# Forgetting attention beside a convolution's layer norm: mean from two partial sums, statistics at the end of their steps, gate exponential one step later

## The reference, cut to what matters

```python
u = a * jax.nn.sigmoid(g)
u = causal_depthwise_conv(u, conv_w, conv_b)              # 31 taps, 512 channels
u = jax.nn.silu(layer_norm(u, conv_ln_g, conv_ln_b))      # mean and variance over the channels
...
for i in range(S // Q_BLOCK):                             # forgetting attention, 8 heads of 64
    logits = q_i @ k[:kl].T * scale + cum[q0:kl, None] - cum[None, :kl]
    p = softmax(where(mask, logits, NEG_INF)); outs.append(p @ v[:kl])
...
return jnp.concatenate([u, att], axis=-1) @ w_out
```

## Time and profile before

| | us |
|---|---|
| median of 3 runs | 1816.08 |
| lowest, highest | 1813.85, 1817.47 |
| the profiled execution | 1815.37 |
| its span in the trace | 1813.6 |
| PE, DVE, ACT, POOL busy | 1773.4, 1029.9, 463.9, 1074.8 |

### The profile page before, as it was taken

The page is one execution under the profiler, slowest core; times in us unless marked ns, Lnnn a source line. Parts: engine busy times, 40 slices in busy tenths (PEclk is TensorE's granted clock), DMA queues, the critical chain, the costliest instruction groups (busy, mean ns, idle before and its releaser), DMA issues.

```text
span 1813.6 us, 22611 instructions
## 1 busy us (share of the span) xinstructions
PE 1773.4 (98%) x8364; PEld 1435.2 (79%) x8364; DVE 1029.9 (57%) x1194; ACT 463.9 (26%) x931; POOL 1074.8 (59%) x604
## 2 busy tenths in 40 slices
PE   9998999999999999999999999999999999999997
PEld 7775777788888877767888888887887888888886
DVE  5999355835252675175625262696766562616177
ACT  6427335401010222163201010212335320202011
POOL 7594452566666665434666666665344566666672
PEclk9999999999999999999999999999999999999999
DMA  6232221233333333211333333332222223333331
GB/s 241 70 100 64 70 82 47 79 96 93 102 95 93 98 100 93 82 47 59 93 98 99 93 94 103 93 93 82 70 70 59 82 93 99 98 93 95 102 93 47
DMA packets 46591, 161.44 MB, mean 89 GB/s; under 512 B 5232, under 2 KB 7792, under 8 KB 46384
## 3 DMA queue, kind: packets, MB, share of 16 engines
q1 hardware_dynamic: 45088, 157.31, 28.5%
q10 hardware_dynamic: 1424, 3.02, 0.5%
HBM read 158.21 MB, written 2.10 MB: 88 GB/s over the span
## 4 chain that ended last, share of the span: by engine, by line
PE 92%; DVE 4%; ACT 2%; issue 1%; POOL 1%; DMA 0%; SPq 0%; DVEq 0%; POOLq 0%; ACTq 0%
PE bank L406 21%; PE bank L407 21%; PE bank L408 21%; PE bank L454 3%; PE bank L455 3%; PE bank L456 3%; PE bank L474 1%; PE bank L476 1%; PE bank L475 1%; PE bank L1002 1%; PE bank L1038 1%; PE bank L1004 1%; PE bank L1003 1%; DVE bank L1773 1%; PE bank L1053 1%
## 5 line engine op out<-in xcount | busy, mean ns | idle before, releaser
L320 POOL TENSOR_TENSOR WL<-RAW,WH 128x1024 fp32r<-128x1024 f32 x291 | 740.8, 2546 | 24.3
L315 POOL TENSOR_SCALAR WH<-RAW 128x1024 fp32r<-128x1024 f32 x291 | 313.2, 1076 | 670.4 <-PE bank L408 363.0
L406 PE MATMUL bank<-AH,WH 128*128 128x512 f32 x848 | 332.6, 392 | 0.0
L408 PE MATMUL bank<-AH,WL 128*128 128x512 f32 x848 | 330.0, 389 | 0.0
L407 PE MATMUL bank<-AL,WH 128*128 128x512 f32 x848 | 330.0, 389 | 0.0
L406 PE MATMUL bank<-HH,WH 128*128 128x512 f32 x832 | 325.2, 391 | 0.0
L407 PE MATMUL bank<-HL,WH 128*128 128x512 f32 x832 | 324.0, 389 | 0.0
L408 PE MATMUL bank<-HH,WL 128*128 128x512 f32 x832 | 323.7, 389 | 0.0
L1428 ACT ACTIVATE TMP<-bank 128x512 f32<-128x512 f32 x96 | 57.3, 596 | 776.9 <-PE bank L408 739.1
L2049 DVE TENSOR_TENSOR HL<-TMP,HH 128x512 fp32r<-128x512 f32 x96 | 239.0, 2490 | 4.0 <-ACT HH L1433 0.7
L2055 DVE TENSOR_TENSOR Y<-Y,bank 128x512 f32<-128x512 f32 x72 | 49.5, 688 | 309.3 <-PE bank L408 309.3
(11 more groups left out here) (390 smaller groups left out, 2355.4 us busy)
## 6 DMA issues: line engine op xcount, KB each, us to landing
RAW<-wstream SPq DMA_DIRECT2D x291, 512.0 KB, 3.5
out<-Y SPq DMA_DIRECT2D x8, 256.0 KB, 2.2
X<-xT SPq DMA_DIRECT2D x3, 512.0 KB, 8.1
TMP<-memT ACTq DMA_DIRECT2D x1, 1024.0 KB, 7.2
MIX<-bands ACTq DMA_DIRECT2D x1, 768.0 KB, 4.6
RAW<-wstream SPq DMA_DIRECT2D x2, 256.0 KB, 3.7
X<-xT SPq DMA_DIRECT2D x2, 256.0 KB, 4.0
BF<-masks ACTq DMA_DIRECT2D x1, 352.0 KB, 4.0
```

The source lines that it names most:

```text
L315: nc.gpsimd.tensor_scalar(WH[:, s, :, :].rearrange("p k n -> p (k n)"), RAW[:, s, :], 1.0, 1.0, ALU.mult, ALU.mult).then_inc(sem("w_high"), 1)
L320: nc.gpsimd.tensor_tensor(WL[:, s, :, :].rearrange("p k n -> p (k n)"), RAW[:, s, :], f32(WH[:, s, :, :].rearrange("p k n -> p (k n)")), A ...
L406: mm(bank, WH[:, slot, k, :], h(k), start=(k == 0), stop=False)
L408: last = mm(bank, WL[:, slot, k, :], h(k), start=False, stop=(k == KT - 1))
```

## The change

Four edits, all in this stage:

1. The sum for the mean is not finished on DVE. At the end of step 3 DVE adds SG[0] and SG[1] into TMP[3] (128 x 512); at the end of step 4 it adds SG[2] and SG[3] into the first tile of Y (128 x 512), in place of L1884 and L1885. PE adds the two by accumulating two products with the matrix of ones.
2. Both statistics products move on PE from between the two groups of transposes to behind the product with V, that is to the end of steps 5 and 7.
3. The subtraction of the mean on DVE and the squares on ACT move from step 5 to step 6; on DVE it stands right behind the maxima of step 6.
4. The gate's exponential on ACT moves from step 9+c to 10+c, and u(c) on DVE from 10+c to 11+c.

```diff
-LN_XC = 5
-LN_SQ = 5
+LN_XC = 6
+LN_SQ = 6
...
-                if i == LN_STAT[0]:
-                    pe.wait_ge(sem("ln_sum"), nth("ln_sum", 1))
-                    mm(B[7][:], ONES[:], TMP[:, 3, :], start=True, stop=True).then_inc(sem("ln_stat"), 1)
-                if i == LN_STAT[1]:
-                    pe.wait_ge(sem("ln_sum"), nth("ln_sum", 2))
-                    mm(B[7][:], ONES[:], TMP[:, 3, :], start=True, stop=True).then_inc(sem("ln_stat"), 1)
                 if 0 <= j < len(fox):
                     fox_transposes(j, 1)
...
                     last.then_inc(sem("fox_pv"), 1)
+                if i == LN_STAT[0]:
+                    pe.wait_ge(sem("ln_sum"), nth("ln_sum", 2))
+                    mm(B[7][:], ONES[:], TMP[:, 3, :], start=True, stop=False)
+                    mm(B[7][:], ONES[:], YTAIL[:, 0, :], start=False, stop=True).then_inc(sem("ln_stat"), 1)
+                if i == LN_STAT[1]:
+                    pe.wait_ge(sem("ln_sum"), nth("ln_sum", 3))
+                    mm(B[7][:], ONES[:], TMP[:, 3, :], start=True, stop=True).then_inc(sem("ln_stat"), 1)
...
-                c = i - LN_GATE - 1
+                c = i - LN_GATE - 2
                 if 0 <= c < 4:
                     act.wait_ge(sem("su_arg"), nth("su_arg", c + 1))
...
+                if i == LN_SUM[0] - 1:
+                    dve.wait_ge(sem("conv"), nth("conv", 2 * CONV_W))
+                    done(v.tensor_tensor(TMP[:, 3, :], SG[:, 0, :], SG[:, 1, :], ALU.add).then_inc(sem("ln_sum"), 1), "ln_sum")
                 if i == LN_SUM[0]:
...
-                    own(v.tensor_tensor(YTAIL, SG[:, 0:2, :], SG[:, 2:4, :], ALU.add).then_inc(sem("dve_step"), 1), "dve_step")
-                    done(v.tensor_tensor(TMP[:, 3, :], YTAIL[:, 0, :], YTAIL[:, 1, :], ALU.add).then_inc(sem("ln_sum"), 1), "ln_sum")
...
+                    done(v.tensor_tensor(YTAIL[:, 0, :], SG[:, 2, :], SG[:, 3, :], ALU.add).then_inc(sem("ln_sum"), 1), "ln_sum")
...
-                c = i - LN_GATE - 2
+                c = i - LN_GATE - 3
                 if 0 <= c < 4:
                     dve.wait_ge(sem("su_done"), nth("su_done", c + 1))
```

More of the change, by code:

```diff
@@ L106 @@
     "al": each(["m1", "mm", "m2", "m3", "b", "f0", "c", "f1"], "al", 8),
-    "sum": [("m1_sum", 7), ("mm_sum", 5), ("ln_sum", 2)] + each(["m2", "m3", "b"], "sum", 7) + each(["f0", "c", "f1", "fin"], "sum", 6),
+    "sum": [("m1_sum", 7), ("mm_sum", 5), ("ln_sum", 3)] + each(["m2", "m3", "b"], "sum", 7) + each(["f0", "c", "f1", "fin"], "sum", 6),
     "stat": each(["m1", "m2", "m3", "b", "f0", "c", "f1", "fin"], "stat", 1),
@@ L1937, in _ @@
                     fox_split((i - 7) // 4)
+                if i == LN_XC:
+                    dve.wait_ge(sem("ln_stat"), nth("ln_stat", 1))
+                    for c in range(4):
+                        done(v.scalar_tensor_tensor(out=SG[:, c, :], in0=B[7][:], scalar=-1.0 / (4 * P), in1=SG[:, c, :],
+                                                    op0=ALU.mult, op1=ALU.add).then_inc(sem("ln_xc"), 1), "ln_xc")
                 conv(TAPS - 3)
```

## The result

| | before | after |
|---|---|---|
| median, us (5 executions each) | 1815.42 | 1823.20 |
| lowest, highest | 1813.85, 1817.47 | 1821.46, 1826.39 |
| the profiled execution | 1815.37 | 1821.46 |
| its span | 1813.6 | 1819.7 |

The ratio is 1.0041, interval 1.0028 to 1.0055: slower, by more than 0.2%. The forecast was 1819.5 and the range ended at 1822.0, so the time lies above it; its sign had been given 0.35. The second measurement (six executions of the changed kernel, 1819.48 to 1825.57) lies just inside the range, by chance of the executions and not by a term of the sum. Before it was run it had been expected at 1821 or more if the lower clock adds to the queues at two places, and at 1819 to 1820 if the first five were high by chance.

A forecast was written before the change was run, and what follows sets the result against it. PE work bounds the span, with DVE leading from about 122 to 187 us. Queue delays and two meetings start the projection 3.4 us late: 1815.37 + 3.4 = 1818.8, or 1819.5 against the median; range 1814.8 to 1822.0.

The forecast's parts named there:

- 2.0 us late: Start of step 8's scores on PE: 1.1 us from step 7's late maxima plus 0.96 for the second statistics product.
- Meetings: Steps 13 and 14: DVE's scalings begin under POOL's L320 and are blocked until it ends, 2.1 and 2.2 us.
- a rival with 0.21: PE's clock falls behind the new step 7 stop, costing some 1.4 us, possibly again ahead of the projection: 1820.9 and up.
- two stops of PE of 3 and 2.5 us: PE waits about 3 us at step 7's product with V and 2.5 us ahead of the output projection.
- no meeting: Rival, steps 13 and 14: DVE's scaling gets in before POOL's L320; +0.7 us, 1816.8 us, chance 0.26.
- A gain: Rival: ACT reaches the squares before DVE needs them, projection starts 1.5 to 4 us earlier; 1814.0 us, chance 0.13.
- (a): Share of the loss named for the experiments: the queue cost of edits 1 to 3 at step 8.
- (b): Share of the loss named for the experiments: the two meetings with POOL that edit 4 leads to.
- (c): Share of the loss named for the experiments: a lower clock behind PE's new stops.

The follow-up runs named there:

- e4: Changed kernel plus products nobody reads on PE, three in the stop of step 7 and two ahead of the projection; 1818.30 us, ratio to before 1.0013.
- e1: Kernel before the change with edit 4 alone (gate's exponential and u(c) one step later); 1818.12 us, ratio to before 1.0010.
- e3: Changed kernel with the second statistics product back ahead of the second head's transposes of step 7; 1818.42 us, ratio to before 1.0012.
- e6: Changed kernel with the subtraction of the mean and the squares back in step 5; 1818.07 us, ratio to before 1.0010.
- e5: Changed kernel with the scalings of the probabilities of blocks 12 and 13 on ACT instead of DVE; 1816.37 us, ratio to before 1.0002.
- h2: Changed kernel with scalings of blocks 12 and 13 on ACT and unread PE products, three in step 7, one in step 12; 1814.13 us, ratio to before 0.9995.
- h1: Kernel before with edit 4, scalings of blocks 12 and 13 on ACT and one unread PE product in step 12; 1812.53 us, ratio 0.9983.
- g1: Kernel before with edit 4 and the scalings of blocks 12 and 13 on ACT; 1813.02 us, ratio to before 0.9990.
- e8: Kernel before with only the scalings of blocks 12 and 13 moved to ACT, as a control; 1815.97 us, ratio to before 1.0003.
- h3: Kernel before with three unread products in PE's 3.55 us stop of step 12; 1816.15 us, ratio to before 1.0004.

## Why the prediction was wrong

Step by step, forecast and trace of after:

- **Edit 1.** Maxima of step 4 1.5 us late, those of step 5 at 145.0: the sum under L320 ran from 139.76 to 141.33, the maxima began at 145.17. Right.
- **Edit 2.** No stop at the channel sum, scores(6) at 147.7: 147.88, no stop. Right.
- **Edit 3.** Squares done at 154.5, DVE waits 1.5, maxima of step 7 at 156.6, product with V at 158.5: 154.43, 1.29, 156.33, 158.26. Right. Then "2.0 us late" at scores(8): 3.0. **This is the step that failed.** The 0.96 us for the second statistic was taken from a row at 2.4 GHz, though the same text let PE stop for 3 us just ahead of it. At the lower clock it took 2.0, and in e4, where the stop was filled, 1.06. By scores(11) the lag was 2.75 (173.06 for 170.31), not 1.4: the statistic's 1.0 and some 0.4 for the work behind it in step 8.
- **Edit 4.** The gate's wait on ACT and the 3.55 us stop gone, the next stop moved to scores(13): right, and these as well as all later times are late by the same 1.5: maxima of step 12 at 182.93 for 181.4, scores(13) at 183.81 for 182.3, last product of u(3) done at 198.51 for 197.0, L637 at 198.62 for 197.1. Meetings 2.16 and 2.36 for 2.1 and 2.2.
- **Behind L637** the forecast added nothing. PE had stopped 1.86 us, the clock fell (0.93, 0.73), and the first part of the projection took 1.4 longer than before. This is a second term that the sum put at nothing. No run fills this stop by itself; the lower clock stands behind it in all four traces that have it (after, e1, e3, e6), and the clock is 1.00 there in the ten that don't.

So: 1818.8 for the profiled execution, with 1.5 and 1.4 added, is 1821.7; it read 1821.46. The mechanism was right as far as the queues and the meetings go. The first missing term had been priced (1.4) and the second named without a price, but both in a rival with 0.21, as if the lower clock were another outcome and not a further term of the same one. The forecast itself had opened two stops of PE of 3 and 2.5 us; the traces are met by the sum of both. The text's own reason against the rival (a lower clock moves POOL's pairs off the scalings) is real but was put at the wrong place. The clock at step 7 delays PE, DVE and POOL alike (step 13's L320 at 188.11 for 186.6, the scaling at 188.39 for 186.9), so the meetings of after stand. Only where the clock falls at the stops of steps 12 and 13 do they part. g0, the same kernel as after, shows it in its profiled execution:

```profile
183.87 1.22 PE L674 MATMUL bank<-MIX 64*128 64x256 f32 x4 [1.85 <-ACT Y L1385]
...
196.60 0.47 PE L637 MATMUL bank<-AH,WH 128*128 128x512 f32 x1
```

Its clock is 0.81 and 0.51 in the two stretches from 180 to 190, its scalings take 0.3 to 0.4 us, and the projection starts 2.4 us behind before's instead of 4.7. One low clock and two meetings stand for each other inside one kernel, and this moves the projection by 2.3 us, its second part by 3.7, from one execution to the next.

The other rivals: *no meeting* (1816.8) is what e5 built, 1816.37. By itself it came in g0 and e4, through the lower clock at steps 12 and 13 and not, as the rival had it, through half a microsecond on DVE or POOL. *A gain* is out: ACT reached the squares when forecast. On the size of the shares, from runs side by side: (a) 1.6 us (h2 less h1), (b) 5.0 with the stop and the lower clock that follow from it (e1 at +2.5 against g1 at -2.4, g0 at +6.0 against e5 at +0.9), and (c) 1.6 (h2's projection against e5's). Edit 4's gain without its cost is 2.4 (g1). 1.6 + 5.0 + 1.6 - 2.4 is 5.8 of the measured 6.0. These shares are not so exact as their sum: e3, e4 and e6 take away 1.5 to 2.6 us each by scores(11) in their traces, and lie 3.2 to 3.4 nearer to before than g0 in the median. The rest, 0.6 to 1.8 us, is within the intervals (each about 1.6 to 2.1 us to either side) and is not explained.

The median of the five executions (7.8 above before) is higher than the second measurement's 6.0; the intervals overlap. The lower clock near 800 us, which only some executions have, is worth about 2 us, enough for such a difference; that it made this one is not shown, since only the fastest of the five was traced.

h1 is the best kernel here: 1812.53, ratio 0.9983 [0.9974, 0.9992]. It is edit 4 and two scalings moved to ACT, with edits 1 to 3 left out. g1, without the unread product, is nearly as good.

## What to carry to other kernels

In this kernel a stop of PE had to be priced twice, with its length and with a lower clock for the work right behind it (1.5 us behind 3.07, 1.4 behind 1.86); if the forecast opens such a stop, the second price belongs in the sum. What is moved earlier meets another engine's schedule: list which instructions then start under a long one that blocks them, as L320 did here, and move those (two scalings to ACT) together with the edit. Edit 4 alone lost 2.5 us (e1), the move alone gained nothing (e8), and the pair gained 2.4 (g1).

## What the runs showed of the hardware

- The length of a stop alone does not tell whether the clock falls. The 2.2 us stop at the channel sum of step 5 never brought the lower level (before, e1, e8, g1, h1, h3: 1.00), while 1.86 us ahead of the projection did in after, e1 and e3 (e1: 0.66 in 195 to 200). Ahead of that stop PE had only scores and transposes, and no filler. The Trainium skill (TensorE: Matmul & The Clock Gate, section "HAM oscillation — how this bites in real kernels") names idle gaps between bursts of products as what lowers the clock. The traces agree in that each fall between 155 and 205 us came behind a stop, and filling the 3.07 us one kept the clock at 1.00 (e4, h2). They also show stops without a fall, and which gap is enough was not settled here.
- The same stops bring it in one execution and not in another: 0.81 and 1.85 us in steps 12 and 13 did in g0, e4 and e6 and did not in after, e1, e3, e5 and g1. With a product placed between (h1, h2) it did not in either trace. A kernel with such stops has a spread of its own, and one profile shows one of its cases.
